# Reciprocal norms and key scales spread by two fp32r products with the identity

## The reference, cut to what matters

```python
def rms_norm(x, g):
    xf = x.astype(jnp.float32)
    y = xf * lax.rsqrt(jnp.mean(xf * xf, axis=-1, keepdims=True) + EPS)
    return (y * g.astype(jnp.float32)).astype(x.dtype)

# latent attention: eight heads of 96 columns, each key row is normalised too
k = jnp.concatenate([k_nope, k_r], axis=-1)
q = rms_norm(q, q_norm_g)
k = rms_norm(k, k_norm_g)
```

## Time and profile before

| | |
|---|---|
| runs | 2774.75, 2777.66, 2782.16 us, median 2777.66 |
| profiled execution | 2783.37 us, of which the span from first to last instruction is 2781.6 us |
| TensorE matmul records busy | 2647.5 us, 95% of the span, 16728 records |
| VectorE | 1578.2 us, 57% |
| ScalarE | 1085.4 us, 39% |
| GpSimd | 983.5 us, 35% |
| mean granted TensorE clock | 0.973 |

### The profile page before, as it was taken

The page is one execution under the profiler, slowest core; times in us unless marked ns, Lnnn a source line. Parts: engine busy times, 40 slices in busy tenths (PEclk is TensorE's granted clock), DMA queues, the critical chain, the costliest instruction groups (busy, mean ns, idle before and its releaser), DMA issues.

```text
span 2781.6 us, 43947 instructions
## 1 busy us (share of the span) xinstructions
PE 2647.5 (95%) x16728; PEld 2340.0 (84%) x16728; DVE 1578.2 (57%) x2426; ACT 1085.4 (39%) x1800; POOL 983.5 (35%) x492
## 2 busy tenths in 40 slices
PE   7998999999899998999999999999989999999998
PEld 5787678888699998888999999989977777788887
DVE  5665523224489885544375663599883353566642
ACT  4445423323442433443345543323324342454532
POOL 2111344444324221112456544443221113564554
PEclk9998999999999999999999999999999899999999
DMA  5220232323222121101322321222111112332223
GB/s 151 64 85 24 68 108 91 98 90 98 68 75 92 54 61 50 45 24 46 122 92 92 107 84 62 90 91 77 54 54 48 31 39 76 121 99 91 91 69 114
DMA packets 61757, 215.27 MB, mean 77 GB/s; under 512 B 8144, under 2 KB 8144, under 8 KB 61584
## 3 DMA queue, kind: packets, MB, share of 16 engines
q1 hardware_dynamic: 49280, 173.63, 19.8%
q10 hardware_dynamic: 11936, 37.99, 4.1%
q0 software_dynamic: 368, 1.23, 0.1%
HBM read 210.65 MB, written 2.16 MB: 77 GB/s over the span
## 4 chain that ended last, share of the span: by engine, by line
PE 38%; issue 26%; POOLq 13%; DVE 11%; DVEq 6%; POOL 2%; ACT 2%; DMA 1%; ACTq 0%
POOLq L605 13%; PE ps L691 9%; PE ps L692 8%; PE ps L693 8%; DVE ps L2529 3%; DVEq L2518 3%; PE ps L1121 2%; PE ps L674 2%; POOL dl L618 2%; DMA dstage<-w_down 1%; PE ps L1096 1%; PE ps L914 1%; PE ps L915 1%; PE ps L916 1%; PE ps L972 1%
## 5 line engine op out<-in xcount | busy, mean ns | idle before, releaser
L604 POOL TENSOR_TENSOR wl<-stage,wh 128x1024 fp32r<-128x1024 f32 x326 | 791.3, 2427 | 1698.6 <-ACT wh L1259 1696.7
L691 PE MATMUL ps<-Uh,wh 128*128 128x264 f32 (+1 forms) x2640 | 894.3, 339 | 29.4 <-DVE Ul L1937 11.7
L692 PE MATMUL ps<-Ul,wh 128*128 128x264 f32 (+1 forms) x2640 | 865.3, 328 | 0.0
L693 PE MATMUL ps<-Uh,wl 128*128 128x264 f32 (+1 forms) x2640 | 862.9, 327 | 0.0
L1259 ACT ACTIVATE wh<-stage 128x1024 fp32r<-128x1024 f32 x326 | 345.4, 1059 | 1047.2 <-PE ps L693 1040.2
L691 PEld LDWEIGHTS ps<-Uh,wh 128*128 128x128 f32 x2640 | 503.5, 191 | 91.3 <-POOL wl L604 12.9
L693 PEld LDWEIGHTS ps<-Uh,wl 128*128 128x128 f32 x2640 | 502.2, 190 | 42.7
L692 PEld LDWEIGHTS ps<-Ul,wh 128*128 128x128 f32 x2640 | 503.9, 191 | 40.1 <-issue 2.4
L2529 DVE SCALAR_TENSOR_TENSOR ps<-arena,v,ps 128x528 f32<-128x528 f32 x232 | 167.9, 769 | 8.3
L692 PE MATMUL ps<-HIDl,wh 128*128 128x512 f32 (+1 forms) x448 | 162.8, 363 | 0.0
L693 PE MATMUL ps<-HIDh,wl 128*128 128x512 f32 (+1 forms) x448 | 162.1, 362 | 0.0
(11 more groups left out here) (366 smaller groups left out, 4812.4 us busy)
## 6 DMA issues: line engine op xcount, KB each, us to landing
stage<-w SPq DMA_DIRECT2D x326, 512.0 KB, 3.6
dstage<-w_down ACTq DMA_DIRECT2D x48, 512.0 KB, 4.4
arena<-bias_rows ACTq DMA_DIRECT2D x16, 448.0 KB, 5.4
arena<-w_mla ACTq DMA_DIRECT2D x8, 384.0 KB, 3.1
H<-xT SPq DMA_DIRECT2D x8, 256.0 KB, 7.0
out<-H ACTq DMA_DIRECT2D x8, 256.0 KB, 2.8
arena<-pT SPq DMA_DIRECT2D x1, 512.0 KB, 8.4
arena<-causal POOLq DMA_DIRECT2D x1, 320.0 KB, 3.3
```

The source lines that it names most:

```text
L604: pool.tensor_tensor(wl[:, j, :], stage[:, j, :], wh[:, j, :].bitcast(F32), ALU.subtract).then_inc(w_split, 1)
L691: pe.matmul(dst, w_lead, tok.part(a_lead, h), start=(k == 0), stop=False)
L692: pe.matmul(dst, w_lead, tok.part(a_rest, h), start=False, stop=False)
L693: mm = pe.matmul(dst, w_rest, tok.part(a_lead, h), start=False, stop=(k == len(acts) - 1))
```

## The change

`invert` and the two other places that make reciprocals follow them with `split_columns`: a drain, a copy that writes the lead in fp32r, a drain, and a subtraction that writes the rest. Both spread places use `column_into` in place of one float32 product: two fp32r products per tile, lead and rest, accumulated, against an fp32r copy of the identity that ScalarE makes once at the start. The key scales go by the same function, straight from the columns of the reciprocals: the diagonal matrices, and the ones that they were multiplied by, are gone.

```diff
+            def column_into(dst, lead, rest, rows, m=P):
+                for x, first in ((lead, True), (rest, False)):
+                    mm = pe.matmul(dst, x[0:rows].to_broadcast([rows, m]), ident_lead[0:rows, 0:rows], start=first, stop=not first)
+                return mm
...
                 for i in range(tok.tiles):
-                    mm = pe.matmul(ps[0:m, bank + i // each, i % each * tok.rows:(i % each + 1) * tok.rows],
-                                   inverses[0:tok.rows, side, i:i + 1].to_broadcast([tok.rows, m]),
-                                   ident[0:tok.rows, 0:tok.rows], start=True, stop=True)
+                    mm = column_into(ps[0:m, bank + i // each, i % each * tok.rows:(i % each + 1) * tok.rows],
+                                     inv_lead[:, side, i:i + 1], inv_rest[:, side, i:i + 1], tok.rows, m)
...
+            pe.wait_ge(ident_ready, 1)
...
                     for i in range(T2.tiles):
-                        mm = pe.matmul(dst, inverses[0:T2.rows, 0, i:i + 1].to_broadcast([T2.rows, P]), ident[0:T2.rows, 0:T2.rows],
-                                       start=True, stop=True)
+                        mm = column_into(dst, inv_lead[:, 0, i:i + 1], inv_rest[:, 0, i:i + 1], T2.rows)
...
                 def key_scales():
                     pe.wait_ge(inv_ready, n.next(inv_ready))
+                    each = T2_TILES // 2
                     for hd in range(2):
-                        yield from unit_steps([ones[0:T2.rows, :]], [diag_of[hd][0:T2.rows]], T2)
+                        b = at["unit"] % 2
+                        at["unit"] += 1
+                        pe.wait_ge(unit_free[b], n.next(unit_free[b]))
+                        for i in range(T2_TILES):
+                            mm = column_into(ps[:, 2 * b + i // each, i % each * T2.rows:(i % each + 1) * T2.rows],
+                                             kscale_lead[:, i, hd:hd + 1], kscale_rest[:, i, hd:hd + 1], T2.rows)
+                        mm.then_inc(unit_done[b], 1)
+                        yield
...
+            act.wait_ge(consts, 1)
+            act.activation(ident_lead[:, :], ident[:, :], ACT.Copy).then_inc(ident_ready, 1)
...
+            def split_columns(x, lead, rest):
+                dve.drain()
+                dve.tensor_copy(lead, x)
+                dve.drain()
+                dve.tensor_tensor(rest, x, lead.bitcast(F32), ALU.subtract)
             def invert(tok, side=0, root=0):
                 dve.wait_ge(rms_ready, n.next(rms_ready))
                 dve.reciprocal(inverses[0:tok.rows, side, 0:tok.tiles], roots[0:tok.rows, root, 0:tok.tiles])
+                split_columns(*(x[0:tok.rows, side, 0:tok.tiles] for x in (inverses, inv_lead, inv_rest)))
                 dve.drain().then_inc(inv_ready, 1)
...
                 dve.reciprocal(inverses[0:T2.rows, :, :], roots[0:T2.rows, :, :])
+                split_columns(*(x[0:T2.rows, :, :] for x in (inverses, inv_lead, inv_rest)))
                 dve.tensor_copy(ropess[0:T2.rows, :], ps[0:T2.rows, 6, 18:18 + 2 * T2_TILES])
                 dve.drain().then_inc(inv_ready, 1)
...
                     dve.reciprocal(qscale[0:META, :, QT - 1:QT], qroots[0:META, :, QT - 1:QT])
-                    dve.drain()
-                    for hd in range(2):
-                        dve.tensor_tensor(diag_of[hd][0:T2.rows].rearrange("p (i c) -> p i c", c=T2.rows),
-                                          ident[0:T2.rows, 0:T2.rows].unsqueeze(1).to_broadcast([T2.rows, T2_TILES, T2.rows]),
-                                          kscale[0:T2.rows, :, hd:hd + 1].to_broadcast([T2.rows, T2_TILES, T2.rows]), ALU.mult)
+                    split_columns(*(x[0:T2.rows] for x in (kscale, kscale_lead, kscale_rest)))
                     dve.drain().then_inc(inv_ready, 1)
```

More of the change, by code:

```diff
@@ L202, in program @@
         smalls = [0]
+        ident_lead = at("ident_lead", [P], dt=F32R)
+        inv_lead, inv_rest = (at(name, [3, T2_TILES], dt=F32R) for name in ("inv_lead", "inv_rest"))
+        kscale_lead, kscale_rest = (at(name, [T2_TILES, 2], dt=F32R) for name in ("kscale_lead", "kscale_rest"))
         def few(*shape):
@@ L340, in program @@
         ksq = za[:, 0, :]
-        diag_of = [W1[6], za[:, 1, :]]
         tails = [W2[5], W1[7]]
@@ L387, in program @@
         inv_ready = sem("inv_ready")
+        ident_ready = sem("ident_ready")
         spread_done = sem("spread_done")
```

## The result

| | median | lowest to highest | runs |
|---|---|---|---|
| before, on the same chip | 2779.91 us | 2774.75 to 2783.17 | 4 |
| after | 2814.24 us | 2806.28 to 2818.00 | 4 |

The ratio is 1.0116 [1.0101, 1.013]: slower by 1.2%, the way that was forecast, but the medians are 34.3 us apart, nearly three times the +11.9 us, and the time lies 4 us outside the range. The profiled execution is the fastest of the four, 2806.28 us with a span of 2804.4; for before they were 2783.37 and 2781.6. Of all the runs in this document one, of e7 (3677 us at a granted clock of 0.648), ran in a slower state of the chip, and is left out of the means and ratios.

A forecast was written before the change was run, and what follows sets the result against it. TensorE was taken to bound the latent attention, VectorE the recurrence and the stretch ahead. Spreads 0, key scales +6.9, VectorE's gain 0, splits +5.0 gave +11.9 us on the median of 2777.66: 2789.6 us, range 2780 to 2810.

The forecast's parts named there:

- The floor of 0.112 us: TensorE's small products: the 128-column weight load sets 0.112 us each, for 88 or 128 columns, fp32r or a float32 record.
- slow fp32r products: Rival on TensorE: under 256 columns fp32r runs at the float32 rate, +29.5 us in all, 2807 us; chance 0.17.
- the faster load: Rival on TensorE: fp32r weights load twice as fast, 0.056 us a product, -8.4 us in all, 2769 us; chance 0.06.
- Spreads, 0 us: Spreads on TensorE: two fp32r products replace two float32 records per tile at equal cost, 0 us for all 126 tiles.
- VectorE's gain, 0 of 6.6: Latent attention, VectorE: dropped multiplications less the split save 6.6 us in all, of which 0 was counted.
- Key scales, +0.45 for a head less some waits: Latent attention, TensorE: 0.89 us a head becomes 1.34; with half clock and waits given back, +6.9 us.
- 7.3 - 0.9 - 1.3: Key scales on TensorE: +7.3 us for 16 heads, less 0.9 and 1.3 us given back by existing waits.
- Splits, +5.0 in ten exposed places: VectorE at the norms: each split adds 0.5 us in 19 places, ten of them exposed, 5.0 us.
- the norm that stood at 762 us: Norm where TensorE already waits for the reciprocal and the normalised input; counted as an exposed split of 0.5 us.
- The six heads: Recurrence heads where VectorE did not wait for the spread and TensorE waits at line 962; splits counted as exposed.
- Four of the 16 groups ran at half clock: Key scales in the latent attention: these four groups pay the added time once more, +1.8 us.
- the rival: Clock in the latent attention: the other twelve key-scale groups fall to half clock, +16 us on the forecast, 2806 us; chance 0.08.

The follow-up runs named there:

- e7: Before, with the key scales' diagonal matrices kept but made fp32r, lead and rest: 2782.76 us, ratio 1.0005.
- e2: After, but with the key scales by diagonal matrices as before, so only the norms' spreads and splits changed: 2791.96 us, ratio 1.0036.
- e4: Before, with the splits of the norms' reciprocals added on VectorE and read by nobody: 2789.94 us, ratio 1.0031.
- e3: Before, with the key scales by float32 columns, one product per tile, no split, norms as before: 2793.80 us, ratio 1.0041.
- e6: Before, with only the new tiles allocated and the identity copied: 2784.39 us, ratio 1.0009.
- e1: After, but with every spread of a norm as before, so only the key scales go by fp32r columns: 2798.74 us, ratio 1.0069.
- e13: After, with the ten query sums of each pair widened to 120 columns: 2786.54 us, ratio to before 1.0020.
- e11: Before, with the ten query sums of each pair widened from 1 to 120 columns: 2773.30 us, ratio 0.9969.
- e9: Before, with eleven unread float32 products of 256 columns in each of the six waits ahead of a recurrence head: 2785.93 us, ratio 1.0012.

## Why the prediction was wrong in size

- **The floor of 0.112 us: right.** Small fp32r products follow each other as float32 records did, 88 and 128 columns alike, and with them fall the rivals of slow fp32r products and of the faster load. The Trainium skill ("TensorE: Matmul & The Clock Gate", weight-path perf modes) ties the fast load to a type that is not FP32; the fp32r loads here are as long as the float32 ones, 192 against 191 ns, and the pace is theirs, so in this kernel fp32r goes like FP32.
- **Spreads, 0 us: right** (e2 against e4, +1.9 with +7 of half clock).
- **VectorE's gain, 0 of 6.6: right.** VectorE is busy for 82.4 us of the first latent stretch, 3.5 less, and TensorE's stretch is longer all the same.
- **Key scales, +0.45 for a head less some waits: about right as their own cost.** At the 0.5 us of the two pairs at full clock, and 0.2 for the first pair of a layer, eight pairs are some 3.5 us (an estimate from three of the eight), and e3 gives 5 to 7; the terms without clock give 7.3 - 0.9 - 1.3 = 5.1.
- **Splits, +5.0 in ten exposed places: wrong.** The added 0.5 us are there at the reciprocal, but of the ten places only the first norm (0.7 us) and the two latent norms (0.4 and 0.2) show them in the time. Around the norm that stood at 762 us after has, in order of time:

```profile
763.61 0.18 DVE L2023 RECIPROCAL small<-small 128x4 f32<-128x4 f32 x1 [2.87 <-ACTq L1415]
763.87 0.17 DVE L2017 CAST inv_lead<-small 128x4 fp32r<-128x4 f32 x1
...
764.37 0.47 PE L730 MATMUL ps<-ident_lead,inv_lead 128*128 128x128 f32 x1 [1.02 <-DVEq L2025]
...
770.14 0.56 PE L694 MATMUL ps<-N1h,wh 128*128 128x264 f32 x1 [3.81 <-DVE N1l L1990]
```

  From the reciprocal to the spread are 0.76 us, where it was 762.04 less 761.77, 0.27: +0.49, as forecast. But from the reciprocal to the first product of the normalised input are 6.53 us against 768.11 less 761.77, 6.34: only +0.2, though the spread ran at half clock on top. The six heads, 3.0 of the 5.0 us, show nothing: their waits kept their 17 us, and from head to head at full clock e4 takes 38.26 us where before takes 38.24. A wait that ends at VectorE does not prove that every step of VectorE is on its chain; I should have followed the chain from the reciprocal to the waiting product.
- **The clock: the step that failed.** The forecast had "Four of the 16 groups ran at half clock ... and pay as much again: +1.8", and the rival gave the clock 0.08 and at most +16 us, of the new groups alone. Measured are 52 us more half clock, some 20 of 32 us (13 to 26 over the range of its price). I counted the lower clock for the changed products, but a fall strikes whatever runs next: in the rows above the projection behind the key scales pays, 0.22 us a product instead of 0.12. And I looked for it in the latent attention only; the splits alone brought 13 us of it (e4), and the stretch ahead of the recurrence, with none of the changed key scales in it, grew by 4.0 us in the profile of after, all but the split's 0.4 by the clock. The clue was in the rows: a stretch with TensorE busy for 242.5 of 250 us had a mean clock of 0.95, so the clock fell there already although TensorE was hardly ever idle, and I read the 0.95 as a constant.
- **The layout: not in the sum.** The new tiles alone cost +2.8 us (e6). What the forecast had without the clock was 10.1 us, and what is left to after without it is 12 (6 to 19); that the two are near each other is in part luck, since the splits came out smaller and the layout was missing.

What stays open: why fp32r columns bring so much more half clock than float32 ones of equal pace (e1 +28, e3 +7), and by which way the unread splits bring 13 us. That the moments at which products follow each other shift against whatever decides on the clock would fit, but no run here tests it; runs of one kernel differ as well (e13's twelve go from 2775.84 to 2801.87 us).

## What to carry to other kernels

A small product costs 0.112 us here, for 88 columns as for 128, in fp32r as in a float32 record; what these have in common is a weight load of 128 columns. Before streaming products are replaced by narrow ones, count loads, not columns. Where TensorE is the full engine and its mean clock is below 1, the clock falls already: here a change in such a place cost nearly three times what its own work was reckoned at, and the work behind it paid. Before idle waits are filled, count a float32 product as two records: the filling here overran its waits and ate what the clock gave back. Columns that fit under the load are nearly free and can hold the clock up: the query sums of 120 columns instead of one took 8.8 us off before, 27 off after, and with the filled waits 12.4 us, a better kernel than both.

## What the runs showed of the hardware

- TensorE falls to half clock in the midst of dense work: in before's profile behind the sums at 1104.5 us, with 9.7 of the 10 us from 1100 to 1110 covered by records (of which those of the sums stream one or two columns each). The Trainium skill ("TensorE: Matmul & The Clock Gate", Part 1) tells of falls behind idle stretches. Filling idle waits did bring the clock back in the recurrence (0.97 to 1.00), so the trace agrees there; in the latent attention it was narrow products that mattered: query sums of 1, 48 (with key sums of 40) and 120 columns gave 0, -15 and -33 us of half clock.
- A microsecond of half clock cost 0.38 us between kernels of the same work (after and e13, before and e11), and 0.37 in the recurrence, where TensorE waits for VectorE once a head (39.40 against 38.24 us from head to head).
- Eleven float32 products of 256 columns leave 22 records and take 4.9 us (e9).
- The same code ran 0.5% slower in the feed-forward stretch when the tiles lay elsewhere in SBUF (300.16 to 301.61 us, e6).
